# Expert-choice table of a fused two-block transformer kernel: side work dealt out singly over a choice's steps, and 84 early blocks in place of 80

## The chip, the cores and the metric

One core of one Trainium2 chip runs the whole program in one launch. The metric is the device time of a run in microseconds (us), lower is better. The kernel before takes 2443.4 us (median of 3 runs, 2443.06 to 2444.09).

## What is computed

The input is 512 tokens of 1024 numbers. A first block does two kinds of attention, merges them, and adds a "peer" layer; a second block does a convolution and state-space mixer. The change is in the peer layer alone:

```python
q = (xt @ w_q).reshape(t, 8, 2, 128)
sc = einsum("thpc,hpnc->thpn", q, sub_keys)          # 16 score rows of 128 for each token
top_s, top_i = top_k(sc, 16)
cand_s = top_s[:, :, 0, :, None] + top_s[:, :, 1, None, :]
best_s, best_pos = top_k(cand_s, 16)                 # 16 of the pairs, for each of 8 heads
gate = softmax(best_s)
hid = gelu(xc . u[idx]) * gate                       # 128 chosen experts for each token
out = sum over the chosen experts of hid * v[idx]
```

There are 16384 experts, each with a row of `u` and one of `v`, 1024 numbers long.

## The kernel before

**Two ways for the tokens.** Tokens 0 to 383 (three tiles, `DT`) are done densely: all 16384 experts are multiplied with all 384 tokens, in 128 blocks of 128 experts, and a table of gates, zero for experts that a token did not choose, is multiplied in. Tokens 384 to 511 (tile `GT`) are done by gathering the chosen rows: POOL fetches one row for each token with an indirect DMA, and VectorE (DVE) forms its product with the token, a "dot" (`Gathered.dot`, L947).

**A block of `u`.** Four engines handle it, in this order:

- SP loads 512 KB into one of three raw buffers (`Early.load`, L873); the load of block n waits until the low half of block n-3 is made.
- ACT makes the high half, `Early.hi` (L887), into one of two buffers; it waits until TensorE is done with block n-2.
- DVE makes the low half, raw minus high half, `Early.lo` (L893), called a "lo" below.
- TensorE (PE) does 24 matmuls of 128x384 (`Early.products`, L904 to L906), ACT takes the Gelu of the sum (L915), and SP stores the result, 192 KB (L879). On ACT the Gelu of block n is followed at once by the high half of block n+2.

**Two phases share the 128 blocks.** `phase_table` computes the first `EARLY` blocks (80) while DVE makes the choices and the gate table; their results go to memory and are read back later. `phase_experts` computes the other `LATE` blocks (48), and for each of the 128 blocks it multiplies in the gates and does 18 matmuls of 128x512 with a block of `v` (L1530 to L1532). There the order of PE is: 6 late blocks ahead, then for each p the block p+6 if it is a late one, and the 18 matmuls of p. The late blocks are p = 0 to 7 and the last 40. The remaining 92 dots and 128 gathered additions are spread over p in proportion to a weight of 8 for a step with a late block and 3 for one without.

**Order of the table phase.** Choice 0 (tile `GT`) with 12 early blocks, choice 1 with 18, choice 2 with 18, the 16 slices of table 0 with 4, choice 3 with 16, the slices of tables 1 and 2 with 4 each, and 4 blocks at the end. The numbers are `E_SCORE`, `E_SLICES` and `E_LAST` in L56. Choices 1 to 3 also hold 12 dots each.

**A choice** is `choose` on DVE: 24 steps. The long ones are runs over the 16 score rows: 16 MAX8 (L1307), 16 pairs of FIND_INDEX8 and MATCH_REPLACE8 (L1312, L1313), 16 MAX8 (L1316), 16 FIND_INDEX8 (L1319); then the same on 8 rows of 80 candidates, the subtraction that releases ACT's exp (L1348), integer operations, and the comparisons of L1372 to L1380. Between the last instruction of a step and the wait for it stands `fill`, which issues los and dots, in turn, up to a count. The count is the share of the choice's cost spent up to that step:

```python
COST = (3.2, 8.5, 3.2, 4.4, 0.3, 1.0, 1.2, 3.3, ...)
spent = [sum(COST[:k + 1]) / sum(COST) for k in range(LINKS)]
share = lambda n, k: [int(n * s) for s in spent][k]
def step(ins):
    link(ins, dots0 + share(DOTS[n], k[0]), e + share(E_SCORE[n], k[0]))
```

So in a choice with 18 blocks and 12 dots the counts after the first steps are 1, 5, 7 and 9 los: four los and two dots stand in a row behind the 8.5 us step. `gates` (L1290 to L1293) is three small instructions, run at the end of choices 2 and 3, after choice 1, and for choice 0 inside choice 1. ACT's program has `exped(n)` at a fixed place among its Gelus: after as many as `share(E_SCORE[n], DIFF) - 2`.

**Queues.** SP issues, strictly in order, the loads of `u`, the stores of early results and the stores of table quarters (`store`, L1138, 2 MB in four pieces). A quarter is stored in the slices stage before the turn of one block, so `early.turn` of the fourth block of that stage, with the load of the block three further on, stands behind the fourth quarter. POOL fetches row s when dot s-5 is done.

Of the kernel before, what the change touches and what calls it, by code (L numbers as in the profile page):

```python
# [27 lines left out]
TT = SEQ // P  # L28
# [14 lines left out]
PH = 8  # L43
# [9 lines left out]


PAIRS = 5 * TOPK
E_SCORE, E_SLICES, E_LAST = (12, 18, 18, 16), 4, 4  # L56
EARLY = sum(E_SCORE) + DT * E_SLICES + E_LAST
LATE = PK - EARLY
DOTS = (0, 12, 12, 12)
# [59 lines left out]
def bc(ap, n):  # L119

    return ap.unsqueeze(len(ap.shape)).broadcast_to(list(ap.shape) + [n])
# [935 lines left out]
def phase_table(c, ijg, early, SC, gat):  # L1057
# [6 lines left out]
    NQ = 2 * PH  # L1064
# [7 lines left out]
    with ExitStack() as ctx:  # L1072
# [11 lines left out]
        at = [0]  # L1084
# [32 lines left out]
        EL = EH2 + E_SLICES  # L1117


        COST = (3.2, 8.5, 3.2, 4.4, 0.3, 1.0, 1.2, 3.3, 1.2, 1.8, 0.2, 0.8, 0.5, 0.3, 0.4, 0.3, 0.3, 0.2, 2.3, 2.3, 1.2, 0.7, 0.4, 0.3)  # L1120
        LINKS, DIFF = len(COST), 10
        spent = [sum(COST[:k + 1]) / sum(COST) for k in range(LINKS)]
        share = lambda n, k: [int(n * s) for s in spent][k]

        @block.sync
        def _(sp):
            def turns(e, n):
                for i in range(n):
                    early.turn(sp, e + i)

            def store(quarter):

                sp.wait_ge(copied, 2 * QSL * (quarter + 1))
                for j in range(PIECES):
                    cut = slice(j * PK // PIECES, (j + 1) * PK // PIECES)
                    quads = slice(j * PK // PIECES // Q_BLK, (j + 1) * PK // PIECES // Q_BLK)
                    src = stage[quarter % 2][:, cut].rearrange("p (a b) t -> p a (b t)", b=Q_BLK)
                    sp.dma_start(t["gates"][quarter, quads].rearrange("a p b t -> p a (b t)"), src).then_inc(early.tabled[quarter % 2], 16)  # L1138

            def stores(tt, e):  # L1140
                for i in range(4):
                    store(4 * tt + i)
                    early.turn(sp, e + i)

            for n in range(3):
                early.load(sp, n)
            turns(E0, EH0)
            stores(0, EH0)
            turns(E3, E_SCORE[3])
            stores(1, EH1)  # L1150
            stores(2, EH2)
            turns(EL, E_LAST)
# [49 lines left out]
        @block.scalar  # L1202
        def _(act):
            def gelus(e, n):
                for i in range(n):
                    early.gelu(act, e + i, EB)

            def exped(n):

                act.wait_ge(gdiff, n + 1)  # L1210
                act.activation(b16, b16, ACT.Exp).then_inc(gexp, 1)

            def turned(n):

                tt = n - 1
                act.wait_ge(t3, n)
                act.activation(ijg[:, :, tt * P:(tt + 1) * P], c.bank[4][:, 0:3 * P].rearrange("p (a b) -> p a b", b=P), ACT.Copy).then_inc(t3o, 1)

            def weigh(j):

                act.wait_ge(hot_made, 2 * j + 2)
                for k in range(ON_ACT):
                    one = hot[0][j % 2][:, k]
                    last = act.activation(one, one, ACT.Copy, scale=ijg[:, 2, j * S + k:j * S + k + 1])
                last.then_inc(weighed_a, 1)

            def slices(tt, e):

                weigh(tt * NSL)
                for s in range(NSL):  # L1230
                    j = tt * NSL + s
                    quarter = j // QSL
                    if s % QSL == 0 and quarter >= 2:
                        act.wait_ge(early.tabled[quarter % 2], 16 * PIECES * (quarter // 2))
                    if s + 1 < NSL:
                        weigh(j + 1)
                    for q in range(2):
                        act.wait_ge(built, 2 * j + q + 1)
                        tok = (2 * s + q) * Q % Q_TOK
                        o = stage[quarter % 2][:, :, tok:tok + Q]  # L1240
                        act.activation(o, c.bank[2 * (s % 2) + q][:].rearrange("p (k i) -> p i k", k=Q), ACT.Copy).then_inc(copied, 1)
                    if s % (NSL // E_SLICES) == NSL // E_SLICES - 1:
                        early.gelu(act, e + s * E_SLICES // NSL, EB)
                        if s == NSL // 2 - 1 and tt < DT - 1:
                            turned(tt + 2)

            def scored(n, e, done=0):

                k = share(E_SCORE[n], DIFF) - 2
                gelus(e + done, k - done)  # L1250
                exped(n)
                gelus(e + k, E_SCORE[n] - k)

            early.hi(act, 0)
            early.hi(act, 1)
            scored(0, E0)
            scored(1, E1)
            gelus(E2, LEAD)
            turned(1)
            scored(2, E2, LEAD)  # L1260
            slices(0, EH0)
            scored(3, E3)
            slices(1, EH1)
            slices(2, EH2)
            gelus(EL, E_LAST)

        @block.vector
        def _(dve):
            count = {"dot": 0, "lo": 0}

            def fill(dots, los):
                while count["dot"] < dots or count["lo"] < los:
                    if count["lo"] < los:
                        early.lo(dve, count["lo"])
                        count["lo"] += 1
                    if count["dot"] < dots:
                        gat.dot(dve, count["dot"])
                        count["dot"] += 1

            def link(ins, dots=0, los=0):  # L1280

                c.steps += 1
                ins.then_inc(c.step, 1)
                fill(dots, los)
                dve.wait_ge(c.step, c.steps)

            def gates(n):
# [8 lines left out]
            def choose(n, e):  # L1296

                dots0, k = count["dot"], [0]

                def step(ins):  # L1300
                    link(ins, dots0 + share(DOTS[n], k[0]), e + share(E_SCORE[n], k[0]))
                    k[0] += 1

                tt = (GT, *range(DT))[n]
                sc = SC[:, tt]
                for j in range(NQ):
                    last = dve.max(t16[:, j, 0:8], sc[:, j])  # L1307
                step(last)
                if n == 1:
                    gates(0)  # L1310
                for j in range(NQ):
                    dve.max_index(i16[:, j, 0:8], t16[:, j, 0:8], sc[:, j])  # L1312
                    last = dve.match_replace(sc2[:, j], t16[:, j, 0:8], sc[:, j], LOWEST)  # L1313
                step(last)
                for j in range(NQ):
                    last = dve.max(t16[:, j, 8:16], sc2[:, j])  # L1316
                step(last)
                for j in range(NQ):
                    last = dve.max_index(i16[:, j, 8:16], t16[:, j, 8:16], sc2[:, j])  # L1319
                step(last)  # L1320
                step(dve.tensor_copy(key, i16.rearrange("p (h f) a -> p f a h", f=2)))

# [9 lines left out]
                step(last)  # L1332
                for h in range(PH):
                    last = dve.max(b16[:, h, 0:8], cand[:, h])
                step(last)
                for h in range(PH):
                    dve.max_index(pos16[:, h, 0:8], b16[:, h, 0:8], cand[:, h])
                    last = dve.match_replace(cand2[:, h], b16[:, h, 0:8], cand[:, h], LOWEST)
                step(last)
                for h in range(PH):  # L1340
                    last = dve.max(b16[:, h, 8:16], cand2[:, h])
                step(last)
                for h in range(PH):
                    last = dve.max_index(pos16[:, h, 8:16], b16[:, h, 8:16], cand2[:, h])
                step(last)

                step(dve.tensor_copy(gs[:, 0], b16[:, :, 0]))
                dve.tensor_tensor(b16, b16, bc(gs[:, 0], TOPK), ALU.subtract).then_inc(gdiff, 1)  # L1348


                one = lambda o, i, by, op: dve.tensor_scalar(part[:, o], i, by, None, op)
# [18 lines left out]
                for f in range(2):  # L1370
                    at_f = where[:, f].rearrange("p (k h) -> p k h", h=PH).unsqueeze(1).broadcast_to([P, TOPK, TOPK, PH])
                    last = dve.tensor_tensor(eqs(f), at_f, over_k(iota16), ALU.is_equal)  # L1372
                step(last)
                for f in range(2):
                    last = dve.tensor_tensor(eqs(f), eqs(f), over_k(key[:, f]), ALU.mult)
                step(last)
                for w in (8 * SLOTS, 4 * SLOTS, 2 * SLOTS):
                    step(dve.tensor_tensor(eq[:, :, 0:w], eq[:, :, 0:w], eq[:, :, w:2 * w], ALU.add))
                two = lambda i: eq[:, :, i * SLOTS:(i + 1) * SLOTS].rearrange("p f (k h) -> p f h k", h=PH)
                step(dve.tensor_tensor(out3[:, 0:2].rearrange("p f (h k) -> p f h k", k=TOPK), two(0), two(1), ALU.add))  # L1380
                assert k[0] == LINKS
                if n == 0:
                    dve.scalar_tensor_tensor(out=gat.idx[:], in0=out3[:, 0], scalar=float(PK), in1=out3[:, 1], op0=ALU.mult, op1=ALU.add).then_inc(gat.ready, 1)
                    return
# [1090 lines left out]
```

## Time and profile before

| | |
|---|---|
| median of 3 runs | 2443.4 us |
| the profiled execution | 2439.86 us, of which the span is 2438.0 us |
| busy in it: PE, DVE, ACT, POOL | 92%, 61%, 34%, 18% |
| mean granted clock of PE | 0.964 |
| table phase | about 574 to 1082 us |
| experts phase | about 1084 to 1815 us |

The span runs from the first to the last instruction of the profiled execution. A row of a timeline gives the start, the duration, the engine, the line, the operation, out<-in, and in brackets how long the engine had been idle before it and what ended that. The duration of a matmul is its latency: the next one starts earlier, so the pace is read from the starts.

### The profile page before, as it was taken

The page shows a single profiled execution, that of the slowest core. Times are in us where ns is not written, and L with a number is a line of the kernel's source. Part 1 is how long each engine was busy: PE and PEld are TensorE (multiplying, and loading weights), DVE is VectorE, ACT ScalarE, POOL GpSimd, SP SyncE. Part 2 cuts the span into 40 slices and gives each one's busy share as a digit, 9 for nine tenths or more (in the row PEclk, how much of TensorE's full clock was granted, in tenths as well). Part 3 has the DMA queues.
Part 4 walks back from the last instruction along what each step waited for, and adds up shares of the span by engine and source line. Part 5 has one row for each costly group of instructions (what it writes and reads, how often), then busy time and mean ns, then how long its engine had stood idle before and what let it go on. Part 6 is the DMA issues. An engine that isn't in the chain of part 4 may idle for free. (4 is left out here: it accounts for less than half of the span.)

```text
span 2438.0 us, 28877 instructions
## 1 busy us (share of the span) xinstructions
PE 2255.0 (92%) x11033; PEld 1874.5 (77%) x11033; DVE 1476.2 (61%) x2645; ACT 819.9 (34%) x1380; POOL 434.0 (18%) x306
## 2 busy tenths in 40 slices
PE   7999999898899888889999999999976999989889
PEld 6777666687899887888888889999965998865444
DVE  3546222426798988847888876888886424334321
ACT  3345212322333645844333333333324322211110
POOL 0100000000211010002323323666650000023000
PEclk9999999899999999999999999999997899989899
DMA  5221233203676584678999997999973222120110
GB/s 210 98 83 53 78 112 130 83 4 94 204 252 219 171 259 131 198 250 312 400 369 370 374 337 251 337 332 344 328 244 126 81 101 90 49 113 35 52 69 35
DMA packets 209690, 449.71 MB, mean 184 GB/s; under 512 B 13585, under 2 KB 132369, under 8 KB 202769
## 3 DMA queue, kind: packets, MB, share of 16 engines
q1 hardware_dynamic: 172688, 313.64, 37.1%
q0 software_dynamic: 36864, 134.23, 15.4%
q8 instruction: 88, 1.44, 0.2%
q14 instruction: 50, 0.40, 0.0%
HBM read 403.78 MB, written 44.04 MB: 184 GB/s over the span
## 5 line engine op out<-in xcount | busy, mean ns | idle before, releaser
L1530 PE MATMUL bank<-Vh,Hh 128*128 128x512 f32 x768 | 299.2, 390 | 2.9 <-DVE Hl L1604 2.8
L1532 PE MATMUL bank<-Vh,Hl 128*128 128x512 f32 x768 | 299.6, 390 | 0.0
L1531 PE MATMUL bank<-Vl,Hh 128*128 128x512 f32 x768 | 299.5, 390 | 0.0
L904 PE MATMUL bank<-XH,Ue 128*128 128x384 f32 x640 | 225.2, 352 | 43.2 <-DVE Ue L893 42.9
L942 POOL DMA_INDIRECT ring<-in_v,gidx x128 | 222.2, 1736 | 161.1 <-DVE x_res L954 69.6
L1550 ACT ACTIVATE Vh<-Vr 128x1024 fp32r<-128x1024 f32 x128 | 135.8, 1061 | 305.8 <-PE bank L1532 300.2
L905 PE MATMUL bank<-XL,Ue 128*128 128x384 f32 x640 | 218.2, 341 | 0.0
L906 PE MATMUL bank<-XH,Ue 128*128 128x384 f32 x640 | 218.1, 341 | 0.0
L1599 DVE TENSOR_TENSOR Vl<-Vr,Vh 128x1024 fp32r<-128x1024 f32 x128 | 156.6, 1223 | 57.5 <-ACT Vh L1550 54.5
L942 POOL DMA_INDIRECT ring<-in_u_rows,gidx x92 | 107.1, 1164 | 410.0 <-DVE ghid L947 235.0
L1530 PEld LDWEIGHTS bank<-Vh,Hh 128*128 128x128 f32 x768 | 144.2, 188 | 33.3 <-DVE Hl L1604 4.6
L1532 PEld LDWEIGHTS bank<-Vh,Hl 128*128 128x128 f32 x768 | 144.1, 188 | 30.3
L1531 PEld LDWEIGHTS bank<-Vl,Hh 128*128 128x128 f32 x768 | 144.1, 188 | 29.1
L904 PEld LDWEIGHTS bank<-XH,Ue 128*128 128x128 f32 x640 | 123.8, 193 | 49.5 <-DVE Ue L893 49.1
L1770 PE MATMUL bank<-X2h,Wh 128*128 128x512 f32 x336 | 132.1, 393 | 6.5 <-DVE Wl L1866 6.5
L904 PE MATMUL bank<-XH,Un 128*128 128x384 f32 x384 | 129.6, 337 | 3.7 <-DVE Un L893 3.7
L1771 PE MATMUL bank<-X2l,Wh 128*128 128x512 f32 x336 | 131.8, 392 | 0.0
L1772 PE MATMUL bank<-X2h,Wl 128*128 128x512 f32 x336 | 131.7, 392 | 0.0
L906 PE MATMUL bank<-XH,Un 128*128 128x384 f32 x384 | 129.3, 337 | 0.0
L905 PE MATMUL bank<-XL,Un 128*128 128x384 f32 x384 | 129.1, 336 | 0.0
L905 PEld LDWEIGHTS bank<-XL,Ue 128*128 128x128 f32 x640 | 123.7, 193 | 0.0
L906 PEld LDWEIGHTS bank<-XH,Ue 128*128 128x128 f32 x640 | 123.2, 193 | 0.0
(335 smaller groups left out, 4764.1 us busy)
## 6 DMA issues: line engine op xcount, KB each, us to landing
Vr<-in_v SPq DMA_DIRECT2D x128, 512.0 KB
W<-in_w_stream SPq DMA_DIRECT2D x26, 2048.0 KB, 8.1
ur<-in_u SPq DMA_DIRECT2D x86, 512.0 KB, 4.7
Gr<-gates SPq DMA_DIRECT2D x32, 768.0 KB, 8.4
XT<-in_u SPq DMA_DIRECT2D x42, 512.0 KB
early<-ar SPq DMA_DIRECT2D x80, 192.0 KB
A<-early SPq DMA_DIRECT2D x80, 192.0 KB
w_raw<-in_w_mixer SPq DMA_DIRECT2D x14, 1024.0 KB
```

The costliest lines, as they stand in the source:

```text
L904: pe.matmul(ps, h[:, k], c.Xh[:, k, 0:DN], start=k == 0, stop=False)
L905: pe.matmul(ps, h[:, k], c.Xl[:, k, 0:DN], start=False, stop=False)
L906: mm = pe.matmul(ps, l[:, k], c.Xh[:, k, 0:DN], start=False, stop=k == KT - 1)
L942: pool.indirect_dma_start(out=self.ring[s % RG], out_offset=None, in_=table, in_offset=at).then_inc(self.landed[s % RG], 16)
L1530: pe.matmul(ps, Hh[r][:, tok], Vh[r][:, cut], start=p == 0, stop=False)
L1531: pe.matmul(ps, Hh[r][:, tok], Vl[r][:, cut], start=False, stop=False)
L1532: mm = pe.matmul(ps, Hl[r][:, tok], Vh[r][:, cut], start=False, stop=p == PK - 1)
L1550: act.activation(Vh[q % RV][:], Vr[q % RR][:], ACT.Copy).then_inc(v_hi, 1)
L1599: dve.tensor_tensor(Vl[q % RV][:], Vr[q % RR][:], Vh[q % RV][:].bitcast(F32), ALU.subtract).then_inc(v_lo, 1)
L1770: pe.matmul(ps, lh, rh, start=k == 0, stop=False)
L1771: pe.matmul(ps, lh, rl, start=False, stop=False)
L1772: mm = pe.matmul(ps, ll, rh, start=False, stop=k == KT - 1)
```

## The change

`TICKS` has one entry for each of 115 places in a choice (each of the 16 or 8 rows of a run is one), with its cost in us, 39.13 in sum. `plan` walks them and places a lo or a dot (1.14 each) as soon as its share is due; `spend` issues them at that place, so inside the runs too. The last row of a run has its place at the step's end, as before. Choice 0 gets 14 blocks instead of 12 and choice 3 gets 18 instead of 16, so `EARLY` is 84 and `LATE` 44, and the experts phase has 8 + 36 late blocks. ACT's exp stands after 9, 12, 12 and 12 Gelus instead of 6, 11, 11 and 9.

```diff
-E_SCORE, E_SLICES, E_LAST = (12, 18, 18, 16), 4, 4
+E_SCORE, E_SLICES, E_LAST = (14, 18, 18, 18), 4, 4
...
-        COST = (3.2, 8.5, 3.2, 4.4, 0.3, 1.0, 1.2, 3.3, 1.2, 1.8, 0.2, 0.8, 0.5, 0.3, 0.4, 0.3, 0.3, 0.2, 2.3, 2.3, 1.2, 0.7, 0.4, 0.3)
-        LINKS, DIFF = len(COST), 10
-        spent = [sum(COST[:k + 1]) / sum(COST) for k in range(LINKS)]
-        share = lambda n, k: [int(n * s) for s in spent][k]
+        TICKS = [*[0.2] * NQ, *[0.52] * NQ, *[0.2] * NQ, *[0.28] * NQ, 0.43, 1.07, *[0.15] * PH, *[0.42] * PH, *[0.15] * PH, *[0.21] * PH,
+                 0.2, 0.25, 0.3, 0.6, 0.5, 0.4, 0.3, 0.25, 0.8, 1.15, 1.15, 1.15, 1.15, 1.14, 0.65, 0.4, 0.6]
+        DIFF, EACH = 4 * NQ + 4 * PH + 3, 1.14
+
+        def plan(los, dots):
+
+            whole = sum(TICKS) + EACH * (los + dots)
+            at, n, out = 0.0, [0, 0], []
+            for cost in TICKS:
+                at += cost
+                for i, (of, ahead) in enumerate(((los, 0.0), (dots, 0.5))):
+                    while n[i] < of and (n[i] + ahead) * whole / of <= at:
+                        n[i] += 1
+                        at += EACH
+                out.append((n[0], n[1]))
+            out[-1] = (los, dots)
+            return out
+
+        plans = [plan(E_SCORE[n], DOTS[n]) for n in range(TT)]
...
-                k = share(E_SCORE[n], DIFF) - 2
+                k = plans[n][DIFF][0] - 2
...
-                    link(ins, dots0 + share(DOTS[n], k[0]), e + share(E_SCORE[n], k[0]))
-                    k[0] += 1
+                def spend():
+                    los, dots = plans[n][k[0]]
+                    k[0] += 1
+                    fill(dots0 + dots, e + los)
+
+                def step(ins):
+                    link(ins, spend)
...
                 for j in range(NQ):
                     last = dve.max(t16[:, j, 0:8], sc[:, j])
+                    if j < NQ - 1:
+                        spend()
                 step(last)
```

The last hunk is repeated in the same form in each of the eight runs, behind the subtraction of L1348, and between the two halves of L1372 and of L1375.

## Rows read from the trace of the kernel before

**Rows 1.** The page, busy time of each engine.

```profile
PE 2255.0 (92%) x11033; PEld 1874.5 (77%) x11033; DVE 1476.2 (61%) x2645; ACT 819.9 (34%) x1380; POOL 434.0 (18%) x306
```

**Rows 2.** Waits (us, times, longest): 574 to 1082 us; the last row choice 1 alone.

```profile
DVE Ue L893 <- ACT Ue L887: 62.2, 35, 7.6
...
PE bank L904 <- DVE Ue L893: 42.9, 16, 7.5
...
DVE Ue L893 <- ACT Ue L887: 11.8, 6, 4.7
```

**Rows 3.** Timeline of DVE: choices 1 and 2 begin; one lo and one dot.

```profile
632.23 3.19 DVE L1307 MAX8 W<-SC 128x8 f32<-128x128 f32 x16
...
647.78 1.26 DVE L893 TENSOR_TENSOR Ue<-ur,Ue 128x1024 fp32r<-128x1024 f32 x1
648.91 1.27 DVE L947 CUSTOM_DVE_ANT_0 XT<-XT,gx 128x1024 f32<-128x1024 f32 x1
...
719.95 3.20 DVE L1307 MAX8 W<-SC 128x8 f32<-128x128 f32 x16
```

**Rows 4.** Timeline of PE: three blocks that begin after idle time, in choices 0, 1, 3.

```profile
590.74 0.44 PE L904 MATMUL bank<-XH,Ue 128*128 128x384 f32 x1 [2.86 <-DVE Ue L893]
...
649.10 0.69 PE L904 MATMUL bank<-XH,Ue 128*128 128x384 f32 x1 [7.53 <-DVE Ue L893]
...
875.11 0.69 PE L904 MATMUL bank<-XH,Ue 128*128 128x384 f32 x1 [5.45 <-DVE Ue L893]
```

**Rows 5.** Busy time by window; then granted clock, DMA share, GB/s.

```profile
576.87:582.00 5.13, 5.13 (x16) 5.13 (x17) 5.10 (x25) 1.15 (x1) 0.00 (x0) 0.50 0.36 102
...
649.10:656.00 6.90, 6.90 (x27) 6.90 (x28) 3.37 (x5) 0.30 (x1) 3.75 (x2) 0.66 0.54 154
```

**Rows 6.** Timeline of ACT and DVE in choice 2, a stretch where PE never waits.

```profile
745.48 0.49 ACT L915 ACTIVATE ar<-bank 128x384 f32<-128x384 f32 x1 [2.72 <-PE bank L906]
745.86 1.05 ACT L887 ACTIVATE Ue<-ur 128x1024 fp32r<-128x1024 f32 x1
746.95 1.23 DVE L893 TENSOR_TENSOR Ue<-ur,Ue 128x1024 fp32r<-128x1024 f32 x1 [2.94 <-ACT Ue L887]
749.64 0.49 ACT L915 ACTIVATE ar<-bank 128x384 f32<-128x384 f32 x1 [2.72 <-PE bank L906]
```

**Rows 7.** Timeline of DVE: row numbers ready, first dot, next step after the gates.

```profile
632.03 0.28 DVE L1383 SCALAR_TENSOR_TENSOR gidx<-out 128x128 uint32<-128x128 f32 x1
...
637.44 1.23 DVE L947 CUSTOM_DVE_ANT_0 XT<-XT,gx 128x1024 f32<-128x1024 f32 x1 [0.90 <-DMA XT<-in_u_rows,gidx]
...
639.48 0.09 DVE L1312 MATCH_VALUE_LOAD W<-W,SC 128x8 f32 x1
```

**Rows 8.** Timeline of ACT in choice 1, behind the exp: Gelu's table, Gelu.

```profile
696.82 1.28 ACT L915 ACT_TABLE_LOAD   x1
698.11 0.49 ACT L915 ACTIVATE ar<-bank 128x384 f32<-128x384 f32 x1
```

**Rows 9.** Timelines of DVE, SP and ACT at the start of choice 3.

```profile
861.26 3.18 DVE L1307 MAX8 W<-SC 128x8 f32<-128x128 f32 x16
...
868.37 4.42 SPq L873 DMA_DIRECT2D ur<-in_u  x1
...
877.12 1.06 ACT L887 ACTIVATE Ue<-ur 128x1024 fp32r<-128x1024 f32 x1 [6.93 <-DMA ur<-in_u]
```

**Rows 10.** Timeline of PE: the slices of tables 0 and 1 begin.

```profile
812.50 0.38 PE L1188 MATMUL bank<-W 128*128 128x128 f32 x1 [2.98 <-ACT W L1224]
...
948.97 0.38 PE L1188 MATMUL bank<-W 128*128 128x128 f32 x1 [2.98 <-ACT W L1224]
```

**Rows 11.** Timeline of PE: a late block begins, and the matmuls behind it.

```profile
1454.43 0.33 PE L904 MATMUL bank<-XH,Un 128*128 128x384 f32 x1
...
1458.61 0.39 PE L1530 MATMUL bank<-Vh,Hh 128*128 128x512 f32 x1
```

**Rows 12.** Busy time by window, steps without a late block; columns as in rows 5.

```profile
1160.00:1440.00 280.00, 280.00 (x1237) 231.86 (x1236) 236.70 (x362) 102.47 (x138) 90.30 (x78) 1.00 1.01 376
```

More of the change, by code:

```diff
@@ L1278, in fill, with link @@
                         count["dot"] += 1
-            def link(ins, dots=0, los=0):
+            def link(ins, then=None):
                 c.steps += 1
                 ins.then_inc(c.step, 1)
-                fill(dots, los)
+                if then is not None:
+                    then()
                 dve.wait_ge(c.step, c.steps)
@@ L1313, in choose @@
                     last = dve.match_replace(sc2[:, j], t16[:, j, 0:8], sc[:, j], LOWEST)
+                    if j < NQ - 1:
+                        spend()
                 step(last)
@@ L1316, in choose @@
                     last = dve.max(t16[:, j, 8:16], sc2[:, j])
+                    if j < NQ - 1:
+                        spend()
                 step(last)
@@ L1319, in choose @@
                     last = dve.max_index(i16[:, j, 8:16], t16[:, j, 8:16], sc2[:, j])
+                    if j < NQ - 1:
+                        spend()
                 step(last)
@@ L1334, in choose @@
                     last = dve.max(b16[:, h, 0:8], cand[:, h])
+                    if h < PH - 1:
+                        spend()
                 step(last)
@@ L1338, in choose @@
                     last = dve.match_replace(cand2[:, h], b16[:, h, 0:8], cand[:, h], LOWEST)
+                    if h < PH - 1:
+                        spend()
                 step(last)
@@ L1341, in choose @@
                     last = dve.max(b16[:, h, 8:16], cand2[:, h])
+                    if h < PH - 1:
+                        spend()
                 step(last)
@@ L1344, in choose @@
                     last = dve.max_index(pos16[:, h, 8:16], b16[:, h, 8:16], cand2[:, h])
+                    if h < PH - 1:
+                        spend()
                 step(last)
@@ L1348, in choose @@
                 dve.tensor_tensor(b16, b16, bc(gs[:, 0], TOPK), ALU.subtract).then_inc(gdiff, 1)
+                spend()
                 one = lambda o, i, by, op: dve.tensor_scalar(part[:, o], i, by, None, op)
@@ L1372, in choose @@
                     last = dve.tensor_tensor(eqs(f), at_f, over_k(iota16), ALU.is_equal)
+                    if f == 0:
+                        spend()
                 step(last)
@@ L1375, in choose @@
                     last = dve.tensor_tensor(eqs(f), eqs(f), over_k(key[:, f]), ALU.mult)
+                    if f == 0:
+                        spend()
                 step(last)
@@ L1380, in choose @@
                 step(dve.tensor_tensor(out3[:, 0:2].rearrange("p f (h k) -> p f h k", k=TOPK), two(0), two(1), ALU.add))
-                assert k[0] == LINKS
+                assert k[0] == len(TICKS)
                 if n == 0:
```

## The prediction

> **What bounds the kernel now.** The page first [rows 1]: PE is busy for 92% of the span and no other engine comes near, so the time is PE's work plus what PE waits. The waits of the table phase come next [rows 2]. The reader is to see two rows that face each other: DVE waits 62.2 us for high halves, and PE waits 42.9 us for low halves. Neither is short of work; they wait in turn. While DVE runs 8.5 us of FIND_INDEX8 and MATCH_REPLACE8 no lo is issued, PE has one block in hand (4.2 us) and runs dry; then DVE issues four los in a row, and each waits for PE to free a buffer. The timeline shows the price at its worst: 7.53 us idle in choice 1, 5.45 in choice 3 [rows 4], and after such a gap the granted clock is low: 27 matmuls take 6.90 us at a mean clock of 0.66 [rows 5], against 27 x 0.173 = 4.7, so 2.2 us more are lost. After the 2.86 us gap the first matmul is 0.44 long, not 0.69, and the pace is kept [rows 4].
>
> **Pace.** One early block of PE: two Gelus of a stretch without PE waits stand 4.16 us apart [rows 6] (24 x 0.173). The low level of the clock, 1.2 GHz: 16 matmuls in 5.13 us, 0.32 each [rows 5], so 7.7 us a block. On DVE a lo or a dot takes 1.14 us from start to start [rows 3].
>
> **The change, part by part.**
>
> *1. Balance of a choice.* A choice's own work is 39.1 us by the ticks. As a check, choice 1 lasts 719.95 - 632.23 = 87.7 us [rows 3]; DVE's waits for high halves in it are 11.8 [rows 2], one wait for a gathered row 0.9 and the gates another 0.9 [rows 7], and 30 fills 34.2, which leaves 39.9. With 18 los and 12 dots DVE needs 73.3 us plus 0.9 for gates; PE needs 18 x 4.16 = 74.9. Choice 0 with 14 los: DVE 55.1, PE 58.2. So even with all 14 or 18 blocks PE is the slower one, narrowly, and a perfect deal leaves only PE's time.
>
> *2. How exact the deal must be.* In steady state [rows 6] the Gelu starts at 745.48, the high half takes 745.86 to 746.9, the lo is done about 748.2, and PE wants it when it ends the block in hand, a matmul's 0.33 us before the next Gelu, at 749.31. A lo may thus start up to 1.1 us late without PE noticing; if it comes early, DVE waits. I walk the plan with this. In a choice of 18 the los end at 1.3, 5.6, 9.3, 13.7, 18.6, 21.8, 25.7, 30.1, 33.8, 37.9, 42.3, 46.1, 50.1, 54.6, 58.3, 62.5, 68.3, 70.5 us of 73.3. An interval over 4.16 adds to the lateness, one under it takes off, never below zero, and what passes 1.1 is PE idle. Choice 0 (intervals 3.4 to 4.3) costs nothing.
>
> *3. Choice 1.* The first dot is planned to start 3.2 us into the choice, but the row numbers are ready at 632.03 and the first row came at 637.44, 5.4 later [rows 7]: DVE waits some 2.0 us, and gates(0) add 0.9 (637.44 + 1.14 to 639.48) before the second lo. With 0.24 from the boundary and 0.14 from the interval lateness is 3.3: 2.2 us of PE idle. The 4.9 interval gives 0.5. The exp: the subtraction now stands right behind the 14th lo; after it ACT runs exp, then loads Gelu's table, 1.28 us, and the Gelu starts with its end [rows 8]. That makes the next high half 0.6 us late; the 5.8 interval before the 17th lo comes on top (0.6 + 0.04 + 1.64 - 1.1): 1.2 us. Sum 3.9.
>
> *4. Choice 2.* 0.4 and 1.2 in the same way, and the boundary (2.8 + 0.9 + 1.14 against 4.16) starts the slices 0.7 later. Sum 2.3.
>
> *5. Choices 0 to 2 together.* From 576.87 to the slices at 812.50 [rows 5, 10] are 235.6 us: 48 blocks (199.7), 2.4 for the slow start [rows 5], 2.98 before the slices, and 30.5 more. Of these I leave 0.9 to the one set of transposes (an estimate) and count 29.6 as gaps and slow clock. Those 29.6 become 6.2; two blocks more are 8.3. Change: -15.1 us.
>
> *6. Choice 3, where the deal does not help.* The idle time at its start is not DVE's: SP issues the load of its third block only at 868.37, behind the 2 MB of the last table quarter, and it lands at 877.12, for which ACT waited 6.93 us [rows 9]. The change makes the second block's lo some 7 us sooner, so PE, which fell idle at 875.11 - 5.45 = 869.7 [rows 4], runs it at once and is dry from 873.8; the third can start at 877.12 + 1.06 + 1.14 + 0.1 = 879.4. From there 16 blocks (66.6), 2.1 of low clock after 5.6 us idle (2.2 in [rows 5]), 2.98, 1.2 and 0.7 as in choice 2: slices at 953.0, against 948.97 [rows 10]. Change: +4.0 us, for two blocks more.
>
> *7. Experts phase.* Four late blocks go: 1458.61 - 1454.43 = 4.18 each [rows 11], on an engine that is never idle there [rows 12]: -16.7 us. Their lo, high half and Gelu go from the same phase to the choices and are counted above. The four results are stored and read back, 8 x 192 KB: the stores lie in the choices, the reads in the middle steps, which have room in time but hardly in share (below). Slices, the last four blocks and all after the experts are unchanged.
>
> *8. A fill in mid-run.* No row shows one. At 635.32 a lo follows 16 MAX8 without a gap, which says nothing; the other end is about 0.1 us, a semaphore's round trip (the three gate instructions take 0.9 us for 0.77 of work). I take 0. At 0.1 for some 100 fills DVE has 10 us more, PE's margin takes 3, 7 remain.
>
> A rule that speaks against this: the Trainium skill ("ScalarE: Activation LUTs", What ACT_TABLE_LOAD costs) prices a change of table at 1.28 us plus a drain of 1.38. By it the block behind the exp would be 1.4 us later in each of choices 1 to 3, an estimate of 4.2 us on top. The trace disagrees: the Gelu starts 1.29 us after the load starts [rows 8].
>
> **Sum.** -15.1 + 4.0 - 16.7 = -27.8 us. Against the profiled execution, 2439.86, that is 2412.1; against the median of the runs, 3.5 higher, 2443.4 - 27.8 = **2415.6 us**.
>
> **Rivals.**
>
> *A. DVE becomes the bound of the choices.* Fills in mid-run cost 0.1 to 0.25 us, or small latenesses do not cancel as in my walk. Against: the sum of ticks agrees with choice 1. For: margin is 0.7 us a choice and 1.1 us a block. 100 fills x 0.1 to 0.2, less 3, are 7 to 17: 2423 to 2432 us. Chance 0.15.
>
> *B. Nearly all gaps close.* The walk overstates 6.2 + 1.9 us of remainders, since ticks are rounded up and DVE gains on them. 2407 to 2410 us. Chance 0.10.
>
> *C. The middle of the experts phase becomes bound by DMA.* It runs at a share of 1.01 and 376 GB/s already [rows 12], and four steps more get 1.5 MB of table-phase results. If nothing can be added, 1.5 MB / 376 GB/s = 4 us, on top of the forecast: 2420 us. Against: PE is busy for all 280 us. Chance 0.05; inside the range.
>
> *D. Slower, by the clock.* The choices become a stream with a small gap at many blocks instead of a few long ones. If such gaps held PE at its low level, a block costs 7.7 instead of 4.16, 3.5 more: over all 68 blocks +240 us. It decides from 8 blocks on (27.8 / 3.5); at 16, 2443 - 28 + 56 = 2472 us. Against: choice 0 has a gap at every second or third block, of 0.25 to 2.9 us, and after 2.86 the matmul pace is kept [rows 4]; my walk leaves seven gaps of 0.4 to 2.2. The Trainium skill ("TensorE: Matmul & The Clock Gate", A second HAM failure mode) describes this case, short idle times between groups of matmuls frequent enough that the clock swings. In this trace only the long gaps show it. Chance 0.04.
>
> **How the numbers follow.** Forecast 0.66, its own range 2411 to 2421. Range 2407 to 2430: B below, A above, C inside, D left out. Faster or slower by over 0.2% (4.9 us), about what a measurement of this kernel can tell from no change: only D is slower, 0.04; no change needs A at three times its price, 0.01; faster 0.95.
>
> **What would show it.** In the table phase, DVE's wait for high halves falls from 62 to 30 us or less, PE's for low halves from 43 to some 15, of which the largest, 5.6 us, stands at the third block of choice 3 with ACT waiting for a load of `u` before it. The slices of table 0 begin near 797.5; from there to those of table 1 it takes 140.5 us instead of 136.5. The granted clock dips once in choices 1 to 3. In choice 1 DVE waits 2 us for the first gathered row. If choices 1 and 2 each last 79 us or more with DVE never idle, A is right; if PE waits in the middle of the experts phase, C is. If choice 3 shows no gap at all, step 6 is wrong.

## The result, and the profile after

The changed kernel takes 2417.5 us (median of 4 runs, 2413.5 to 2419.3) against 2443.2 before; the ratio is 0.9896, 95% interval 0.9884 to 0.9908. The forecast was 2415.6, -27.8 us; measured are -25.7. The profiled execution took 2416.6 us with a span of 2414.8. Its times below are therefore to be set against the 2438.0 of the span before, a difference of 23.2.

The page's line of busy times and the waits from 574 to 1082 us of the changed kernel (us, times, longest), to be read beside [rows 1, 2]:

```profile
PE 2248.3 (93%) x11033; PEld 1871.5 (78%) x11033; DVE 1478.5 (61%) x2645; ACT 820.3 (34%) x1380; POOL 436.8 (18%) x306
```

```profile
DVE Ue L893 <- ACT Ue L887: 37.6, 29, 7.5
...
PE bank L904 <- DVE Ue L893: 21.0, 7, 7.1
...
ACT Ue L887 <- DMA XT<-in_u: 6.8, 2, 6.4
```

The two rows that faced each other have both halved: DVE's wait for high halves from 62.2 to 37.6, PE's wait for los from 42.9 to 21.0, in 7 places instead of 16 (the first of the seven, 7.07 us, is the wait for the first block and stood before as well). PE's own timeline shows which places are left: the first block, one at the start of choice 1, one in the last third of each of choices 1, 2 and 3, one at the third block of choice 3, and (as before) one among the last four early blocks. The rows of L1203 are the first matmuls of tables 0 and 1.

```profile
574.28 0.69 PE L904 MATMUL bank<-XH,Ue 128*128 128x384 f32 x1 [7.07 <-DVE Ue L893]
...
641.01 0.44 PE L904 MATMUL bank<-XH,Ue 128*128 128x384 f32 x1 [2.49 <-DVE Ue L893]
...
706.32 0.45 PE L904 MATMUL bank<-XH,Ue 128*128 128x384 f32 x1 [1.04 <-DVE Ue L893]
...
782.85 0.45 PE L904 MATMUL bank<-XH,Ue 128*128 128x384 f32 x1 [1.04 <-DVE Ue L893]
...
794.43 0.38 PE L1203 MATMUL bank<-W 128*128 128x128 f32 x1 [2.98 <-ACT W L1239]
...
860.92 0.63 PE L904 MATMUL bank<-XH,Ue 128*128 128x384 f32 x1 [5.15 <-DVE Ue L893]
...
922.05 0.44 PE L904 MATMUL bank<-XH,Ue 128*128 128x384 f32 x1 [1.03 <-DVE Ue L893]
...
933.65 0.58 PE L1203 MATMUL bank<-W 128*128 128x128 f32 x1 [2.98 <-ACT W L1239]
```

Cut at PE's starts, the span falls into six stretches. The table gives their lengths in us, for all kernels of this study (the experiments behind the second row are described below); each column comes from the timeline of PE. "Choices 0-2" runs from the first early block to the first matmul of table 0, "to table 1" from there to the first of table 1 (choice 3 lies in it), "to experts" from there to the first late block, "experts" to the last matmul of that phase.

| kernel | up to the first early block | choices 0-2 | to table 1 | to experts | experts | behind them |
|---|---|---|---|---|---|---|
| before | 576.9 | 235.6 | 136.5 | 135.4 | 730.2 | 623.4 |
| changed | 574.3 | 220.1 | 139.2 | 138.4 | 717.8 | 624.9 |
| changed, second profile | 574.9 | 219.9 | 139.4 | 138.4 | 719.0 | 620.5 |
| new deal, 80 early | 576.0 | 220.8 | 137.9 | 136.6 | 730.2 | 623.6 |
| old clumps, 84 early | 574.0 | 243.7 | 139.6 | 135.4 | 716.9 | 624.7 |
| new deal, 88 early | 576.7 | 236.8 | 146.3 | 137.3 | 700.4 | 624.3 |
| load first | 576.0 | 219.9 | 134.7 | 131.3 | 716.7 | 626.1 |
| dot later | 575.7 | 218.4 | 138.7 | 136.5 | 716.2 | 625.5 |
| quarter block first | 577.0 | 220.9 | 140.3 | 135.0 | 717.6 | 625.5 |
| these three | 577.0 | 218.5 | 133.2 | 130.0 | 715.8 | 624.3 |
| dots due by steps | 576.8 | 220.6 | 140.3 | 138.4 | 710.0 | 617.5 |
| all four | 574.7 | 217.5 | 133.8 | 130.9 | 710.3 | 617.0 |
| all but the quarter block | 577.0 | 218.4 | 133.5 | 132.3 | 710.3 | 616.9 |

The first column holds nothing that any edit touches and still moves between 574.0 and 577.0. The others are steadier: the two profiles of the changed kernel agree to 0.2 us in the three columns behind it and to 1.2 in the experts phase, but differ by 4.4 in the last.

So the change took 15.5 us off choices 0 to 2 (forecast 15.1) and 12.4 off the experts phase (forecast 16.7). It put 2.7 on the stretch with choice 3 (forecast 4.0) and 3.0 on the one behind it, for which the forecast had none. Two things were thus to be found out: whether the mechanism is the one I named, and what took 4.3 + 3.0 us back.

The 3.0 us go with TensorE's granted clock. At the start of a table PE stands still for 2 to 4 us, and the mean clock from 1 us ahead of the first matmul of table 1 to 11 us behind it is 1.00, 0.86 or 0.72. The time from there to the first matmul of table 2 falls into three groups by it, whatever else was edited:

| mean clock at table 1 | profiles | table 1 to table 2, us |
|---|---|---|
| 1.00 | before, old clumps, quarter block first, these three | 55.8 to 56.0 |
| 0.86 | new deal with 80 and with 88, load first, dot later, all four, all but the quarter block | 56.7 to 57.2 |
| 0.72 | changed (both), dots due by steps | 58.0 |

Before had 1.00 there and the changed kernel 0.72, which is 2.0 us. From table 2 to the first late block it is 79.4 us at 0.86 (before) and 80.4 at 0.72 (changed), the other 1.0.

### The profile page after: what moved, and what is told of

Its sections match the earlier page's. It is cut to its first block and busy times, and to the rows that moved or that the text cites. A ratio compares the mean times of both kernels' runs of the same rounds, so it can differ in the third digit from the quotient of the medians.

```text
span 2414.8 us, 28885 instructions
## 1 busy us (share of the span) xinstructions
PE 2248.3 (93%) x11033; PEld 1871.5 (78%) x11033; DVE 1478.5 (61%) x2645; ACT 820.3 (34%) x1380; POOL 436.8 (18%) x306
## 3 DMA queue, kind: packets, MB, share of 16 engines
q0 software_dynamic: 36864, 134.23, 15.5%
## 5 line engine op out<-in xcount | busy, mean ns | idle before, releaser
L904 PE MATMUL bank<-XH,Ue 128*128 128x384 f32 x672 | 233.3, 347 | 21.0 <-DVE Ue L893 21.0
L906 PE MATMUL bank<-XH,Ue 128*128 128x384 f32 x672 | 228.2, 340 | 0.0
L905 PE MATMUL bank<-XL,Ue 128*128 128x384 f32 x672 | 228.1, 339 | 0.0
L904 PEld LDWEIGHTS bank<-XH,Ue 128*128 128x128 f32 x672 | 129.0, 192 | 23.1 <-DVE Ue L893 23.1
L905 PEld LDWEIGHTS bank<-XL,Ue 128*128 128x128 f32 x672 | 129.1, 192 | 0.0
L906 PEld LDWEIGHTS bank<-XH,Ue 128*128 128x128 f32 x672 | 128.7, 191 | 0.0
L904 PE MATMUL bank<-XH,Un 128*128 128x384 f32 x352 | 119.0, 338 | 5.3 <-DVE Un L893 5.3
L1203 PE MATMUL bank<-W 128*128 128x128 f32 x768 | 100.8, 286 | 21.5 <-ACT W L1239 20.7
L1436 DVE TENSOR_TENSOR W<-tab_sb,ijg 128x1024 f32<-128x1024 f32 x96 | 113.1, 1220 | 9.8 <-PE bank L1203 9.8
```

Of the source, the lines that this page charges most:

```text
L904: pe.matmul(ps, h[:, k], c.Xh[:, k, 0:DN], start=k == 0, stop=False)
L905: pe.matmul(ps, h[:, k], c.Xl[:, k, 0:DN], start=False, stop=False)
L906: mm = pe.matmul(ps, l[:, k], c.Xh[:, k, 0:DN], start=False, stop=k == KT - 1)
```

## The experiments

Each was timed beside the kernel before on the same chip, on three chips in all. The kernel before took 2441.8 us beside the first four kernels below, 2442.5 beside the next four and 2440.8 beside the last three; across these groups the ratios are to be compared, not the times.

**The changed kernel again**, no edit.

> The changed kernel once more, on the chip of the next three. Both theories: 2417 us, within 2413 to 2420. If the spread of its runs comes from the granted clock behind the 2.98 us gap ahead of each slices stage, as I think, the profile shows in those three places a level that need not be the one of the first profile (0.73 over 11 us at tables 1, 0.58 over 7 us at table 2, 1.00 at table 0). If it comes from DMA, those places look the same and the gap of 3.3 us early in the experts phase has another size.

Measured: 2419.3 us (2414.0 to 2420.5), ratio 0.991, interval 0.9895 to 0.9925. At the three tables the idea of a level that changes from profile to profile found no support: the windows that begin 1 us ahead of tables 0 and 1 and 4.0 us ahead of table 2 show the same levels in both profiles (1.00, 0.72, 0.72). At another place it holds. Behind the gap at the start of choice 1, 2.49 us in the first profile and 2.33 in the second, the clock was low in the first and full in the second (columns: length, PE, PEld, DVE, ACT, POOL busy, granted clock, DMA share, GB/s):

```profile
641.00:648.00 7.00, 6.99 (x31) 7.00 (x32) 6.86 (x33) 0.93 (x2) 1.69 (x2) 0.76 0.98 383
```

```profile
641.49:648.49 7.00, 6.75 (x37) 6.43 (x38) 6.86 (x33) 1.44 (x2) 1.70 (x2) 1.00 1.01 393
```

The gaps early in the experts phase have other sizes in the second profile: 0.16 for 1.61 us and 2.65 for 2.95. So neither of the two ideas alone fits the spread, and the 2.7 us by which this profile is shorter lie behind the experts phase (620.5 us for 624.9), where neither looked. The first profile at the tables:

```profile
793.43:805.43 12.00, 10.48 (x81) 10.08 (x82) 11.57 (x13) 8.61 (x26) 0.00 (x0) 1.00 0.00 1
932.65:944.65 12.00, 11.00 (x65) 11.01 (x66) 9.71 (x11) 7.07 (x22) 0.00 (x0) 0.72 0.00 0
987.65:999.65 12.00, 9.02 (x48) 8.70 (x47) 7.29 (x9) 7.94 (x21) 0.00 (x0) 0.72 0.77 236
```

**One part at a time.** The new deal with the old number of blocks:

```diff
-E_SCORE, E_SLICES, E_LAST = (14, 18, 18, 18), 4, 4
+E_SCORE, E_SLICES, E_LAST = (12, 18, 18, 16), 4, 4
```

> The new deal with the old 80 early blocks (12, 18, 18, 16). My theory, gaps of PE closed by the deal: choices 1 and 2 as in the changed kernel; choice 0 becomes bound by DVE (52.8 us against 49.9 of PE), so from PE's first early block to the first slices about 215 us, 20 less than before; choice 3 hardly changes, since its gap waits for a load of u. In all 2422 us. Rival, that the move of four blocks is what brings the gain: 2435 us.

Measured: 2426.8 us, ratio 0.9939 (0.9926 to 0.9953), 15.0 less than the 2441.8 of before on that chip, where 20 were expected. The rival's 2435 is out. Choices 0 to 2 took 220.8 us, not 215. With 12 blocks PE stops in choice 0, once for 2.55 us, where the changed kernel has no gap, and the first gathered row costs more. It is there 8.65 us after POOL began to fetch it (631.32 to 639.97), against 6.02 in the changed kernel (632.37 to 638.39); why is open. DVE waits 5.87 us for it, PE stands still for 5.75, and the first matmul behind is 0.69 long:

```profile
639.97 1.23 DVE L947 CUSTOM_DVE_ANT_0 XT<-XT,gx 128x1024 f32<-128x1024 f32 x1 [5.87 <-DMA XT<-in_u_rows,gidx]
```

```profile
642.59 0.69 PE L904 MATMUL bank<-XH,Ue 128*128 128x384 f32 x1 [5.75 <-DVE Ue L893]
```

The same 220 us hold 48 blocks here and 50 in the changed kernel: the two blocks that choice 0 got cost nothing there.

**The old clumps with the new number**, the kernel before with

```diff
-E_SCORE, E_SLICES, E_LAST = (12, 18, 18, 16), 4, 4
+E_SCORE, E_SLICES, E_LAST = (14, 18, 18, 18), 4, 4
```

> 84 early blocks with the old clumped fills. My theory: the four moved blocks cost PE as much in the choices as they save in the experts phase, less what they fill of the gaps by chance: 2441 us, between 2437 and 2444. Rival, that early blocks are cheap because they lie in idle time: 2427 us.

Measured: 2437.1 us (2434.2 to 2441.1 in 10 runs), ratio 0.9981 (0.9971 to 0.999): 4.7 less, at the lower edge of what I gave and far from the rival's 2427. Choices 0 to 2 grow by 8.1 us for two blocks, the experts phase falls by 13.3. The long gaps stand as in [rows 4]:

```profile
654.80 0.69 PE L904 MATMUL bank<-XH,Ue 128*128 128x384 f32 x1 [7.49 <-DVE Ue L893]
```

So the deal alone is worth 15.0, the number alone 4.7, both 22.5 on that chip. Most of it is the deal. On top of it the number brings 7.5 instead of 4.7; the intervals are some 3 us wide, so that it pays more there is not shown.

**88 early blocks.**

```diff
-E_SCORE, E_SLICES, E_LAST = (14, 18, 18, 18), 4, 4
+E_SCORE, E_SLICES, E_LAST = (15, 19, 19, 19), 4, 4
```

> The new deal with 88 early blocks (15, 19, 19, 19). My theory: PE already sets the pace of every choice, so a block moved there costs what it saves (4.16 against 4.18 us); DVE gets 3 us of margin a choice, so the 1.04 us gaps shrink. 2416 us, between 2413 and 2420, no change from the changed kernel. Rival 1, idle time is left in the choices: another 10 us less, 2407. Rival 2, DVE or DMA is the limit: 2422 us or more.

Measured: 2421.3 us (2417.1 to 2423.6), ratio 0.9911 (0.9896 to 0.9926), against 0.991 for the changed kernel: no gain, as expected of choices that PE already paces, though 1.3 us above the range I gave and close to what rival 2 says. The waits decide against that rival: DVE waits 53.7 us for high halves in the table phase, more than the 37.6 of the changed kernel, so it is PE that is waited for. One point fell: the gaps of 1.04 grew to 1.56 instead of shrinking. With 19 los the places in the plan are others, and probably the uneven interval decides, not DVE's margin. Choices 0 to 2 grew by 16.7 us, where three blocks are 12.5. Of the other 4.2, a new gap in choice 0 is 1.5, the two grown ones 1.0, more time at the low clock 1.1, while the gap at the start of choice 1 gives 0.6 back (1.92 for 2.49); 1.2 stay open.

**The load of u ahead of the quarter.** SP's order in `stores`; `turned` is `turn` without its load:

```diff
                 for i in range(4):
+                    early.load(sp, e + i + 3)
                     store(4 * tt + i)
-                    early.turn(sp, e + i)
+                    early.turned(sp, e + i)
```

> The changed kernel with SP issuing each load of u ahead of the table quarter that stood before it. My theory, the 5.2 us gap at the third block of choice 3 is that load behind 2 MB of stores: the gap and the slow clock behind it go, 6 to 7 us, and the 3.1 us gap of the last four early blocks, which has the same cause, shrinks: 2409 us against 2417. Rival, the load waits for bandwidth and not for its place: 2416 us, the gap stays.

Measured: 2407.1 us (2403.0 to 2408.5), ratio 0.9854 (0.9839 to 0.9869). The gap at the start of choice 3 falls from 5.15 to 1.46 us and the matmul behind it is 0.44 long, not 0.63:

```profile
862.88 0.44 PE L908 MATMUL bank<-XH,Ue 128*128 128x384 f32 x1 [1.46 <-DVE Ue L897]
```

That stretch falls by 4.5 us and the next by 7.1, of which 5.0 lie in the last four early blocks. The load waited for its place behind the quarter; the rival, by which the gap stays, is out. (Issued sooner, the load also no longer runs beside the quarter's transfers; what of the wait is order and what is sharing is not told apart. 0.9 of the 7.1 go with the clock at table 1, 0.86 here.) What is left has moved to the other transfer of the same queue: in this kernel ACT waits 4.83 us for a result of the early blocks to be stored, also behind a quarter:

```profile
859.42 0.49 ACT L919 ACTIVATE ar<-bank 128x384 f32<-128x384 f32 x1 [4.83 <-DMA early<-ar]
```

**The first dot later.**

```diff
-                for i, (of, ahead) in enumerate(((los, 0.0), (dots, 0.5))):
+                for i, (of, ahead) in enumerate(((los, 0.0), (dots, 1.0))):
```

> The changed kernel with the first dot of each choice due half a share later (1.0 instead of 0.5), when its row has landed. My theory: DVE's wait of 3.2 us in choice 1 goes, and PE's gap of 2.5 us behind it too: 2415 us against 2417. Rival, that gap is the gates' and the interval's, not the row's: 2417 us, the gap stays at 2 us or more.

Measured: 2415.0 us (2412.8 to 2416.3), ratio 0.9891 (0.9875 to 0.9906). The time is as expected, though the difference from the changed kernel is inside the intervals; the profile is clearer. DVE has no wait for a gathered row and PE no gap at the start of choice 1, where the changed kernel had 3.24 and 2.49. Choices 0 to 2 gain only 1.7 us, since the shifted dots lengthen another interval: the gap of 1.04 late in the choice is 1.62 now.

```profile
692.52 0.44 PE L904 MATMUL bank<-XH,Ue 128*128 128x384 f32 x1 [1.62 <-DVE Ue L893]
```

**A quarter of a block ahead of the slices.** In PE's slices loop:

```diff
                     j, r = tt * NSL + s, s % 2
+                    early.products(pe, e + s * E_SLICES // NSL, EB, s % (NSL // E_SLICES), NSL // E_SLICES)
                     pe.wait_ge(weighed_a, j + 1)
...
-                    early.products(pe, e + s * E_SLICES // NSL, EB, s % (NSL // E_SLICES), NSL // E_SLICES)
```

> The changed kernel with PE doing the quarter of an early block ahead of the matmuls of each slice, not behind them, so that the 2.98 us gap ahead of each slices stage becomes 1.9. My theory: 1 us saved three times, and the granted clock does not fall at any of the three places, which cost the changed kernel 3.0 us more than the kernel before in its profile: 2417 - 3 - 3 = 2411 us and a narrower spread of runs. Rival, the level there has nothing to do with the gap: 2414 us or more, and low clocks at the slices as before.

Measured: 2417.4 us (2415.0 to 2418.6), ratio 0.9896 (0.9881 to 0.9911): no gain, a miss in the time. In the mechanism it is half right. The clock did not fall in any of the three windows (columns as above):

```profile
796.92:808.92 12.00, 10.46 (x81) 10.07 (x82) 11.57 (x13) 8.60 (x26) 0.00 (x0) 1.00 0.00 0
937.24:949.24 12.00, 10.46 (x81) 10.07 (x82) 11.57 (x13) 8.60 (x26) 0.00 (x0) 1.00 0.00 1
992.24:1004.24 12.00, 10.00 (x76) 9.60 (x77) 9.79 (x11) 9.37 (x27) 0.00 (x0) 1.00 0.72 223
```

and the stretch behind table 1 is 3.4 us shorter. But the 1 us three times was never to be had: DVE is busy 11.57 of 12 us at the start of a table and sets when the slices begin, so a quarter block done in PE's gap probably saves nothing that DVE does not take again. And what was won is in part given back: PE comes sooner to the third block of choice 3, whose load still stands behind the last quarter of table 0. ACT waits 8.10 us for it (6.42 in the changed kernel) and PE 6.83 (5.15); among the last four early blocks PE waits 4.18 (3.13).

```profile
862.72 1.06 ACT L887 ACTIVATE Ue<-XT 128x1024 fp32r<-128x1024 f32 x1 [8.10 <-DMA XT<-in_u]
```

```profile
865.08 0.69 PE L904 MATMUL bank<-XH,Ue 128*128 128x384 f32 x1 [6.83 <-DVE Ue L893]
```

**The three together.**

> The three edits together. My theory: they act in different places and add up, 2409 - 2 - 6 = 2401 us. Rival, part of it is given back in the experts phase by transfers that now meet: 2406 us or more.

Measured: 2401.2 us (2399.1 to 2402.7), ratio 0.9832 (0.9819 to 0.9846). As expected, though by other shares: 10 from the loads, 2 to 3 from the dot. The rest, some 3 us, can't be told from the spread of the stretches. That the quarter block pays once the load no longer stands behind the table would fit; the last two experiments try it.

**Where the experts phase lost 4 us.** The changed kernel's PE stops 2.95 us in the eighth step of that phase, where it stopped 0.12 before:

```profile
1148.81 0.50 PE L1571 MATMUL bank<-Vh,Hh 128*128 128x512 f32 x1 [2.95 <-DVE Hl L1645]
```

Its DVE just before:

```profile
1141.46 1.22 DVE L947 CUSTOM_DVE_ANT_0 ring<-ring,gx 128x1024 f32<-128x1024 f32 x1
...
1142.60 1.22 DVE L947 CUSTOM_DVE_ANT_0 ring<-ring,gx 128x1024 f32<-128x1024 f32 x1
...
1144.75 1.22 DVE L947 CUSTOM_DVE_ANT_0 ring<-ring,gx 128x1024 f32<-128x1024 f32 x1 [0.92 <-DMA ring<-in_u_rows,gidx]
...
1146.57 1.23 DVE L947 CUSTOM_DVE_ANT_0 ring<-ring,gx 128x1024 f32<-128x1024 f32 x1 [0.59 <-DMA ring<-in_u_rows,gidx]
...
1148.19 0.55 DVE L1645 TENSOR_TENSOR Hl<-A,Hh 128x384 fp32r<-128x384 f32 x1
```

Four dots in one step of 4.1 us, with the low half that PE needs behind them; 1.5 of the 2.95 us are DVE's waits for two gathered rows among them. The kernel's weights give 8 to p = 6 and 7, but the late blocks of PE stand in p = 0 and 1. With 80 early blocks `due` rises by 3 and 3 there; with 84 the sum of weights is 574 instead of 594, 220 x 34 / 574 is 13.03 instead of 12.59, and it rises by 3 and 4.

That is not all of it. Another gap, of 1.61 us (none before, 0.16 in the second profile), stands 24 us into the phase. It is the case of choice 3 again: on SP the load of `u` stands behind two loads of gates whose issue takes 11.54 us (9.66 before), and ACT waits for it.

```profile
1074.12 11.54 SPq L1524 DMA_DIRECT2D Gr<-gates  x2
1085.77 3.82 SPq L873 DMA_DIRECT2D XT<-in_u  x1
```

```profile
1093.91 1.06 ACT L887 ACTIVATE Un<-XT 128x1024 fp32r<-128x1024 f32 x1 [2.87 <-DMA XT<-in_u]
```

```profile
1096.28 0.44 PE L904 MATMUL bank<-XH,Un 128*128 128x384 f32 x1 [1.61 <-DVE Un L893]
```

The two gaps are 4.4 us more than before, which is the 4.3; the clock behind both is full in this profile.

The edit weights the step in which PE does the block:

```diff
-        work = [8 * max(lates[p + 1] - LEAD, 0) + 3 * (p + 1 - max(lates[p + 1] - LEAD, 0)) for p in range(PK)]
+        ups = [lates[min(p + 1 + LEAD, PK)] - LEAD for p in range(PK)]
+        work = [8 * ups[p] + 3 * (p + 1 - ups[p]) for p in range(PK)]
```

> The changed kernel with the dots and additions of the experts phase weighted by the step in which PE really does a late block (p = 0, 1 and 86 to 121), not by the number of the block. My theory: the 3 us gap of PE in the eighth step comes from 3 and then 4 dots put into two steps of 4.1 us, one dot more than with 80 early blocks; it goes with the slow clock behind it (some 1.5 us), and the three gaps at the end (0.8, 1.7, 1.2 us) shrink too: the experts phase takes 712 us instead of 718, the kernel 2412 against 2418. Rival, the gap is the gathered rows' traffic meeting the table and v loads: it moves to steps 0 and 1, and the phase stays at 717 us or more.

Measured: 2402.9 us (2396.9 to 2405.5), ratio 0.9836 (0.9822 to 0.9851), 15 less than the changed kernel where I expected 6. The phase takes 710.0 us, with no gap of PE in it but the one at its start and one of 0.45 us; the three at the end, 2.6 us in sum, which the kernel before had too (2.8), are gone as well. The other half lies behind it, and I had not seen it: in the changed kernel DVE still has additions of gathered rows to do when PE is through, and PE waits for the norm behind them. First the changed kernel, then this one:

```profile
PE bank L252 <- DVE HN L1743: 30.6, 1, 30.6
```

```profile
PE bank L252 <- DVE HN L1744: 22.5, 1, 22.5
```

The last steps hold 1 or 2 additions now instead of 3 or 4.

**All four, and all but the quarter block.**

> This edit and the three of the run before together. If they add up: 2401 - 6 = 2395 us.

> The same without the quarter block ahead of the slices. If that edit only keeps the clock up at the slices, which cost 3.4 us in the stage behind table 1 and came to nothing in the whole, this is 2397 us, 1 to 3 more than with it; if it is worth nothing at all, 2395, the same.

Measured: 2386.0 us (2379.9 to 2386.2), ratio 0.9763 (0.9749 to 0.9778), with all four; 2388.7 (2385.5 to 2390.3), ratio 0.9781 (0.9768 to 0.9795), without the quarter block. Both are 8 to 9 below what I expected, as the weights alone were, since their part behind the experts phase was not in the sums. The first is the fastest kernel of the study, 31 us below the changed one. The quarter block may be worth 2.7 us; the intervals overlap, so this stays open.

## Why the prediction was right, point by point

- **Step 1, balance.** Right. PE paces the choices with 14 or 18 blocks, and 88 early blocks bring nothing. DVE's real work follows the ticks: from the first lo of choice 2 to the first one behind the choice (712.53 to 788.87) are 76.3 us, and DVE is busy for 74.1 of them, against 73.3 + 0.9 reckoned. The margin is as narrow as forecast.
- **Steps 2 to 5, the walk with a slack of 1.1 us.** The mechanism is right; the closeness of the sum, 220.1 us against 235.6 - 15.1 = 220.5, is luck in part. The gaps are 2.49 (forecast 2.2), 1.04 and 1.04 (forecast 1.2 each), 4.6 in sum where the walk had 6.2; the 1.7 us lost to the low clock behind the 2.49 gap, which the walk did not have, make up for it. The second profile has 219.9 with full clock there and 0.7 more of gaps. Of the small ones, 0.5 in choice 1 and 0.4 in choice 2, the first is there in the second profile (0.44) and the second in neither, though the interval that should bring it is (4.90 us, los at 724.96 and 729.86). So the walk's slack was probably a little too small. The 2.2 at the start of choice 1 rests on two errors: the row came 6.6 us after the instruction that makes the row numbers began (631.78 to 638.39), not 5.4, so DVE waited 3.24 us and not 2.0; and the gates, 0.9, stand behind the second lo (L1306 at 641.96, the lo at 639.74), not ahead of it. The experiment that moved that dot shows the wait for the row as the cause of the gap: it went.
- **Step 6, choice 3.** Right, and the cause is shown. Gap 5.15 (forecast 5.6) with the clock low behind it, the stretch +2.7 (forecast +4.0). In the changed kernel too ACT waited for the load:

```profile
858.55 1.06 ACT L887 ACTIVATE Ue<-XT 128x1024 fp32r<-128x1024 f32 x1 [6.42 <-DMA XT<-in_u]
```

- **Step 7, experts.** Mis-sized: -16.7 forecast, -12.4 in the profile, -13.3 in the kernel that changed the number alone. "On an engine that is never idle there" was read from a window [rows 12] that begins behind the place where the rounding of `due` struck. The four blocks did go, at 4.18 each; what came back is 2.95 us of gap behind the fourth dot in one short step and 1.61 behind a load of `u`. The line "Slices, the last four blocks and all after the experts are unchanged" belongs to this step and failed as well. The slices of tables 1 and 2 ran 3.0 us longer with the lower clock, a term that the sum had at nothing. What lies behind the experts phase was 1.5 longer in this profile and 2.9 shorter in the second, so nothing is shown there.
- **Step 8, a fill in mid-run.** Right to take nothing. The lo starts 0.24 us behind the start of a MATCH_REPLACE8 that is followed after 0.19 otherwise, so 0.05 us here:

```profile
720.01 0.08 DVE L1334 MATCH_VALUE_LOAD W<-W,SC 128x8 f32 x1
720.08 0.29 DVE L1334 FIND_INDEX8 W<-W,SC 128x8 uint32<-128x128 f32 x1
...
720.34 0.28 DVE L1335 MATCH_REPLACE8 W<-W,SC 128x128 f32<-128x128 f32 x1
720.58 1.23 DVE L893 TENSOR_TENSOR Ue<-ur,Ue 128x1024 fp32r<-128x1024 f32 x1
721.72 1.22 DVE L947 CUSTOM_DVE_ANT_0 SC<-SC,gx 128x1024 f32<-128x1024 f32 x1
...
722.87 0.09 DVE L1334 MATCH_VALUE_LOAD W<-W,SC 128x8 f32 x1
```

- **The price of the exp.** The trace after agrees with the one before: the Gelu starts 1.29 us after its table load does. The second charge of 1.38 us that the Trainium skill names ("ScalarE: Activation LUTs", What ACT_TABLE_LOAD costs) is not there.

```profile
692.24 1.28 ACT L915 ACT_TABLE_LOAD   x1
693.53 0.49 ACT L915 ACTIVATE ar<-bank 128x384 f32<-128x384 f32 x1
```

- **The total.** The four stretches that the sum is made of give -22.2 us in the profile, not -27.8. The medians give -25.7: 1.1 more come from the first and last stretch, which no edit was to change, and 2.5 from the profiled runs, of which that of before was 3.4 us below its median and that of the changed kernel 0.9. So the total came out closer than its parts, and that is luck.
- **The signs.** DVE's wait for high halves fell to 37.6, not to 30, and PE's for low halves to 21.0, not 15, of which 7.07 are the first block's. Table 0 began at 794.4 (forecast 797.5), in a profile whose first block is 2.6 us earlier. The clock was to dip once in choices 1 to 3; it dipped twice in the first profile (behind the gaps of 2.49 and 5.15 us) and once in the second.
- **Rivals.** A: out, DVE waits for high halves in all choices (1.55 us in choice 2). B: out, the gaps of 1.04 stand. C: the middle is as before, PE busy for all of 285 us at a DMA share of 1.02. The waits for gathered rows of 0.9 and 0.6 us above and the 1.61 behind the gates' loads are at the start of the phase. D: out. The mean granted clock from the first early block to table 0 was 0.98, and behind the gaps of 1.04 it was full. But a first matmul of 0.44 us, from which the forecast read that the pace is kept [rows 4], does not say so by itself: behind the gap of 2.49 us it was 0.44 long as well, and the mean clock over the next 7 us was 0.76. The swinging clock of the Trainium skill ("TensorE: Matmul & The Clock Gate", A second HAM failure mode) did not come with the small gaps here.

## What to carry to other kernels

Where two engines wait for each other in turn over a shallow buffer, deal the small one's work out at the other's pace and walk the intervals against the slack, which was reckoned here as 1.1 us of 4.16; beyond the point where one engine paces the stage, more work moved into it brought nothing. A stall at the start of a stage can be another queue's order: the same load issued ahead of 2 MB of stores was worth 10 us. Weights that spread side work must follow the step in which the main engine has time, up to the last one, for what is left at the end stands alone behind it; and a changed count moves their rounding.

## What was not expected of the hardware

A gap of PE of the same 2.98 us ahead of a table was followed by the full clock in some kernels and by a lower mean in others. Over the windows from 1 us ahead of the first matmul of tables 0 and 1 to 11 us behind it, in the profiles of before, changed and the experiments, there are 15 places with that gap: the mean clock was 1.00 in 7 and 0.86 or 0.72 in 8. With gaps of 3.36 us (dot later, all but the quarter block) it was 1.00 at table 0 and 0.86 at table 1, in both; with 2.34 us (the three together, all four) 1.00 at both tables of the one and 0.86 at both of the other; with 1.94 us (quarter block first) 1.00 at both. So a forecast can count on neither level at such a gap. By the table above it costs 2 us at table 1 at the most; what decides is open.

Ahead of early blocks, in the 7 us behind a gap, the mean clock was 1.00 at every gap of up to 1.86 us. It was 0.76 at one of 1.92 and one of 2.49 us, but 1.00 at six of 2.24 to 2.55 and at two of 2.86 and 3.01. At all gaps over 3.05 us it was 0.80 or less.

The runs of one kernel spread by 1.1 us (new deal with 80 blocks, 5 runs) up to 8.6 (dots due by steps, 5 runs); those of the kernel before by 5.6 in 14 runs on one chip and by 6.5 in 9 on another. The number of early blocks does not order this, and it was not tried further.
